# Experts' loops on one core: bounds loaded once, addresses computed early, loop hints, and gate and up as 256 columns with the sum over channels in two banks

## The reference, cut to what matters

```
expert of a token: the best of 4 groups, in it the 2 best of 8 experts   (1024 tokens, 32 experts)
hid = silu(x @ w_gate[e]) * (x @ w_up[e])      # x 1024 channels, hid 512
y   = hid @ w_down[e]                          # 1024 channels
out = sum over a token's two experts of weight * y
```

## Time and profile before

| | |
|---|---|
| median of three runs | 4520.54 us |
| the profiled execution | 4520.74 us, its span 4519.0 us |
| TensorE busy | 3849.0 us, 85% |
| VectorE busy | 1608.9 us, 36% |
| ScalarE busy | 905.4 us, 20% |
| granted TensorE clock, mean | 0.959 |
| DMA, mean over the span | 143 GB/s |
| first to last record of L2387 and L2396, layer 0 | 2471 to 3157 us |
| the same, layer 1 | 3746 to 4434 us |

### The profile page before, as it was taken

One profiled execution on the slowest core, in us unless ns is written; L12 is line 12 of the kernel. 1 busy time (PEld: TensorE's weight loads), 2 busy tenths in 40 slices (PEclk: granted clock), 3 DMA queues, 4 the chain that ended last, 5 costly groups with the idle time before them and its releaser, 6 DMA issues.

```text
span 4519.0 us, 113553 instructions
## 1 busy us (share of the span) xinstructions
PE 3849.0 (85%) x45324; PEld 2478.6 (55%) x45325; DVE 1608.9 (36%) x3673; ACT 905.4 (20%) x2284; POOL 271.6 (6%) x453
## 2 busy tenths in 40 slices
PE   6997888999998899999897777777699987877774
PEld 3564665554445554446644666666444446766664
DVE  2676666223106641524634222222411142222214
ACT  3013444111003321311522111111200021111111
POOL 0000000000000000000001111111100002111111
PEclk9998999999999999999998999999799998999997
DMA  8101223002100001102413778885300225778784
GB/s 318 38 19 57 94 96 120 22 24 68 39 37 1 1 10 47 45 30 94 164 44 139 297 319 326 347 337 217 112 37 37 76 97 234 296 288 364 322 348 141
DMA packets 94346, 644.30 MB, mean 143 GB/s; under 512 B 18640, under 2 KB 41240, under 8 KB 60752
## 3 DMA queue, kind: packets, MB, share of 16 engines
q10 hardware_dynamic: 28896, 386.28, 20.5%
q1 hardware_dynamic: 46928, 194.98, 11.6%
q0 software_dynamic: 18336, 60.44, 4.1%
HBM read 594.70 MB, written 46.92 MB: 142 GB/s over the span
## 4 chain that ended last, share of the span: by engine, by line
PE 48%; issue 5%; DVE 4%; DVEq 2%; DMA 2%; ACT 1%; POOLq 0%; POOL 0%; SPq 0%; ACTq 0%
PE banks L258 22%; PE banks L2387 14%; PE banks L2396 7%; DVEq L2290 1%; DMA arena<-y_tok,arena 1%; PE banks L2382 1%; PE banks L1519 1%; PE banks L2378 1%; DVE arena L2525 1%; DVE arena L1634 1%; PE banks L2118 1%; DVEq L2525 1%; DMA h_tok<-arena 0%; PE banks L467 0%; PE banks L1568 0%
## 5 line engine op out<-in xcount | busy, mean ns | idle before, releaser
L258 PE MATMUL banks<-arena 128*128 128x512 f32 (+2 forms) x4544 | 1749.4, 546 | 38.8 <-ACTq L137 16.9
L258 PEld LDWEIGHTS banks<-arena 128*128 128x128 f32 x4544 | 840.3, 191 | 935.9 <-issue 885.0
L2387 PE MATMUL banks<-arena 128*32 128x128 f32 x20480 | 658.7, 280 | 138.2 <-issue 130.2
L2387 PEld LDWEIGHTS banks<-arena 128*32 128x32 f32 x20480 | 571.9, 112 | 208.4 <-issue 206.7
L2396 PE MATMUL banks<-arena 128*32 128x128 f32 x10240 | 341.7, 290 | 168.6 <-DVE arena L2525 168.3
L2396 PEld LDWEIGHTS banks<-arena 128*32 128x32 f32 x10240 | 301.8, 117 | 207.5 <-issue 206.4
L2490 DVE COPY arena<-banks 128x128 f32 x162 | 47.2, 291 | 491.4 <-PE banks L2382 488.2
L1588 PE MATMUL banks<-arena 128*64 128x128 f32 x1952 | 161.7, 284 | 55.1 <-ACT arena L1601 39.4
L945 DVE SCALAR_TENSOR_TENSOR arena<-arena 128x1024 f32<-128x1024 f32 x240 | 195.9, 878 | 0.2 <-DVEq L137 0.2
L2353 POOL DMA_INDIRECT arena<-h_tok,arena x176 | 171.9, 977 | 142.2 <-POOL arena L2350 136.5
L301 DVE SCALAR_TENSOR_TENSOR arena<-banks,arena 128x512 f32<-128x512 f32 (+1 forms) x72 | 51.9, 721 | 333.2 <-PE banks L258 333.2
(11 more groups left out here) (327 smaller groups left out, 3257.6 us busy)
## 6 DMA issues: line engine op xcount, KB each, us to landing
arena<-in_w_gu ACTq DMA_DIRECT2D x120, 2048.0 KB, 7.4
arena<-in_w_dn ACTq DMA_DIRECT2D x60, 2048.0 KB
arena<-in_w_ada SPq DMA_DIRECT2D x24, 2048.0 KB, 7.3
y_tok<-arena SPq DMA_DIRECT2D x648, 32.0 KB
arena<-in_w_gu SPq DMA_DIRECT2D x8, 2048.0 KB, 9.2
y_tok<-arena POOLq DMA_DIRECT2D x1, 12800.0 KB, 36.0
arena<-in_ab_w_ada SPq DMA_DIRECT2D x6, 2048.0 KB, 9.7
arena<-in_cd_w_ada SPq DMA_DIRECT2D x6, 2048.0 KB, 7.2
```

What stands on the lines that cost most here:

```text
L258: last = pe.matmul(self.bank_of(g, n), lhsT, rhs, start=k == 0, stop=k == KT - 1)
L2387: last = pe.matmul(bank(2 + part)[32 * q:32 * q + 32, 0:128], xbT[:, 128 * j + 32 * q2:128 * j + 32 * q2 + 32], w_gu[slot][part][:, 2 * q2 ...
```

## The change

The weights of gate and up are laid out anew on the host: unit j holds the channels of half j for all columns, 256 columns (128 of gate, 128 of up) for each strip. A matmul streams 256 columns, a block has 32 instead of 64 of them. The sum over the channels ends in two banks: half 0 in bank 2, half 1 in bank 3. ScalarE copies bank 2 to gu_part, VectorE adds bank 3 to it, ScalarE takes SiLU of 128 columns, VectorE multiplies 128 columns. Addition, SiLU and product of block b - 1 now all stand in turn b. In the loops VectorE computes addresses ahead of its waits (snap), and bounds are loaded once and handed on as registers. TensorE's loops have the hint at the back edge. ScalarE issues the gate/up loads when half 1 of the last block is done.

```diff
-        w_gu = [[mem(a + UNIT * h, KT, 4, 128) for h in range(2)] for a in SLOTS]
+        w_gu = [[mem(a + UNIT * j, 16, 256) for j in range(2)] for a in SLOTS]
+        gu_part = mem(HT + 4992, 256)
+        gu_sum = mem(HT + 5248, 256)
...
             def in_turn(self, eng, first, second):
-                first(0, 0)
+                c0, c1 = self.cum(eng, 0), self.cum(eng, 1)
+                first(0, 0, c0, c1)
                 with eng.Fori(0, E // 2 - 2) as p:
-                    first(2 * p + 1, 1, p)
-                    second(2 * p, 0, p)
-                    first(2 * p + 2, 0, p + 1)
-                    second(2 * p + 1, 1, p)
+                    c1, c2 = self.cum(eng, 2 * p + 1), self.cum(eng, 2 * p + 2)
+                    first(2 * p + 1, 1, c1, c2, p)
+                    c0 = self.cum(eng, 2 * p)
+                    second(2 * p, 0, c0, c1, p)
+                    c3 = self.cum(eng, 2 * p + 3)
+                    first(2 * p + 2, 0, c2, c3, p + 1)
+                    second(2 * p + 1, 1, c1, c2, p)
...
+            def trips(self, eng, begin, end):
+                return nc.Fori(begin, end, engines=bass.OrderedEngineSet([eng.engine]), hint_back_edge=True)
...
-            def gu_half(self, pe, slot, part, j):
+            def gu_half(self, pe, slot, j):
                 for q2 in range(4):
                     for q in range(4):
-                        last = pe.matmul(bank(2 + part)[32 * q:32 * q + 32, 0:128],
-                                         xbT[:, 128 * j + 32 * q2:128 * j + 32 * q2 + 32], w_gu[slot][part][:, 2 * q2 + j, q],
-                                         start=j == 0 and q2 == 0, stop=j == 1 and q2 == 3, tile_position=(0, 32 * q),
+                        last = pe.matmul(bank(2 + j)[32 * q:32 * q + 32, 0:256],
+                                         xbT[:, 128 * j + 32 * q2:128 * j + 32 * q2 + 32], w_gu[slot][j][:, 4 * q2 + q],
+                                         start=q2 == 0, stop=q2 == 3, tile_position=(0, 32 * q),
                                          skip_group_check=True)
...
                 def gate_up(i, slot, begin, end, nth=None):          # TensorE
...
+                    with self.trips(pe, begin, end) as b1:
                         pe.wait_ge(self.x0, b1)
-                        pe.wait_ge(self.ma, b1)
-                        self.gu_half(pe, slot, 0, 0)
+                        pe.wait_ge(self.pc, b1)
+                        self.gu_half(pe, slot, 0).then_inc(self.g0, 1)
+                        pe.wait_ge(self.mu, b1)
+                        self.turn_hid(pe)
                         pe.wait_ge(self.x1, b1)
-                        self.gu_half(pe, slot, 0, 1).then_inc(self.ga, 1)
-                        pe.wait_ge(self.mb, b1)
-                        self.turn_hid(pe)
                         pe.wait_ge(self.xr[1], b1)
                         self.turn_x(pe).then_inc(self.xt[1], 1)
-                        self.gu_half(pe, slot, 1, 0).then_inc(self.gb0, 1)
-                        self.gu_half(pe, slot, 1, 1).then_inc(self.gb, 1)
+                        self.gu_half(pe, slot, 1).then_inc(self.g1, 1)
...
             def blocks_act(self, a):
+                def silu(b1):
+                    a.wait_ge(self.ad, b1)
+                    return a.activation(sg, gu_sum[:, 0:128], ACT.Silu).then_inc(self.si, 1)
+
+                def gate_up(i, slot, begin, end, nth=None):
+                    with a.Fori(begin, end) as b1:
+                        silu(b1)
+                        a.wait_ge(self.g0, b1)
+                        a.activation(gu_part, bank(2)[:, 0:256], ACT.Copy).then_inc(self.pc, 1)
+                    a.wait_ge(self.g1, end)
+                    a.sem_inc(passed, 1)
...
             def blocks_dve(self, d):
+                def add(b1):
+                    d.wait_ge(self.g1, b1)
+                    d.wait_ge(self.pc, b1)
+                    d.tensor_tensor(gu_sum, gu_part, bank(3)[:, 0:256], ALU.add).then_inc(self.ad, 1)
+
+                def times(b1):
+                    d.wait_ge(self.si, b1)
+                    d.tensor_tensor(hid, sg, gu_sum[:, 128:256], ALU.mult).then_inc(self.mu, 1)
+
+                def gate_up(i, slot, begin, end, nth=None):
+                    with d.Fori(begin, end) as b1:
+                        add(b1)
+                        self.turned_half(d, 1).then_inc(self.x1, 1)
+                        times(b1)
+                        self.keep_hid(d, b1)
+                        d.wait_ge(self.he, b1)
+                        d.wait_ge(self.xt[1], b1)
+                        self.turned_half(d, 0).then_inc(self.x0, 1)
+                        at = d.snap(((b1 + 1) & (XB - 1)) * 256)
+                        d.wait_ge(self.x_ok[2], b1)
+                        d.tensor_copy(xr, xb[:, bass.ds(at, 256)]).then_inc(self.xr[1], 1)
...
                 def down(i, slot, begin, end, nth=None):             # VectorE
                     with d.Fori(begin, end) as b1:
-                        at = ((b1 + 1) & (HELD - 1)) * 128
+                        at = d.snap(((b1 + 1) & (HELD - 1)) * 128)
                         d.wait_ge(self.dm, b1)
```

More of the change, by code:

```diff
@@ L2407, in blocks_pe @@
                 self.turn_x(pe).then_inc(self.xt[0], 1)
-                def gate_up(i, slot, nth=None):
+                def gate_up(i, slot, begin, end, nth=None):
                     nth = i // 2 if nth is None else nth
-                    begin, end = self.cum(pe, i), self.cum(pe, i + 1)
                     pe.wait_ge(self.wa[slot], 16 * nth + 16)
@@ L2464, in gate_up, with down @@
                             self.load_gu(a, slot, e, part)
-                def down(i, slot, nth=None):
-                    with a.Fori(self.cum(a, i), self.cum(a, i + 1)) as b1:
-                        room = (b1 & (XB - 1)) * 256
+                def down(i, slot, begin, end, nth=None):
+                    with a.Fori(begin, end) as b1:
+                        room = a.snap((b1 & (XB - 1)) * 256)
                         a.wait_ge(self.yf, b1)
@@ L2476, in down @@
                         self.load_dn(a, slot, self.expert(a, i + 2))
-                self.in_turn(a, gate_up, down)
-                down(E - 1, 1)
-                top = self.cum(a, E)
+                begin, top = self.in_turn(a, gate_up, down)
+                a.wait_ge(self.ad, top)
+                a.sem_inc(passed, 1)
+                silu(top)
+                down(E - 1, 1, begin, top)
                 for half in (self.y0, self.y1):
@@ L2488, in keep_hid @@
             def keep_hid(self, d, b1):
+                at = d.snap((b1 & (HELD - 1)) * 128)
                 d.wait_ge(self.ht, b1)
-                d.tensor_copy(held[:, bass.ds((b1 & (HELD - 1)) * 128, 128)], bank(4)[:, 0:P]).then_inc(self.he, 1)
+                d.tensor_copy(held[:, bass.ds(at, 128)], bank(4)[:, 0:P]).then_inc(self.he, 1)
             def blocks_dve(self, d):
                 d.sem_inc(self.yf, 6)
-                d.sem_inc(self.ma, 1)
+                d.sem_inc(self.g1, 1)
                 d.sem_inc(self.dm, 1)
@@ L2509, in gate_up @@
+                def times(b1):
+                    d.wait_ge(self.si, b1)
+                    d.tensor_tensor(hid, sg, gu_sum[:, 128:256], ALU.mult).then_inc(self.mu, 1)
+                def gate_up(i, slot, begin, end, nth=None):
+                    with d.Fori(begin, end) as b1:
+                        add(b1)
+                        self.turned_half(d, 1).then_inc(self.x1, 1)
+                        times(b1)
                         self.keep_hid(d, b1)
-                        d.wait_ge(self.sa, b1)
@@ L2527, in down @@
                         d.tensor_copy(hidS[:, 64:128], held[:, bass.ds(at + 64, 64)]).then_inc(self.h1, 1)
-                self.in_turn(d, gate_up, down)
-                top = self.cum(d, E)
-                d.wait_ge(self.sb, top)
-                d.sem_inc(passed, 1)
-                d.tensor_tensor(hid[:, 64:128], sg[:, 64:128], bank(3)[:, 64:128], ALU.mult).then_inc(self.mb, 1)
+                begin, top = self.in_turn(d, gate_up, down)
+                add(top)
+                times(top)
                 self.keep_hid(d, top)
```

52 lines of the change are left out of this document (16 added, 36 removed).

## The result

The changed kernel takes **4354.97 us** (median of 4 runs, 4341.51 to 4363.8), against 4523.07 for the kernel before: ratio 0.9626, 95% interval 0.9596 to 0.9656. The forecast was 4316, in a range of 4265 to 4400. The profiled execution took 4360.02 us, its span is 4358.2 us.

A forecast was written before the change was run, and what follows sets the result against it. No engine is full; TensorE's 22% idle, at loop changes and a piece after the gather, was the prize. Columns 6, idle piece 45, loop changes 123, addresses 21, clock 20, less loads 10: 205 off 4520.7 gives 4316 us, range 4265 to 4400.

The forecast's parts named there:

- Columns and idle piece: Gate/up turns: 256-column matmuls save 6 us, and the longer queue bridges TensorE's idle piece after the gather, 45 us.
- Changes of loop: Between gate/up and down loops: fewer bound loads and VectorE leaving the gate/up loop earlier save 123 us.
- The late ScalarE: Light gate/up to heavy down: ScalarE issues two weight loads first, returns y late, costing the second down block 0.35 us.
- Early addresses: Down loop: the address of held computed ahead of VectorE's wait removes 0.22 us per further block, 21 us.
- The hint: Jump back of TensorE's loops: named with the early addresses, but given no saving or cost of its own.
- Clock: Phases behind changes of loop: about half the clock dips vanish with the shorter idle, 20 us back.
- Loads: Expert weight loads: pairs with 4 blocks outrun the DMA queues, so 10 us are subtracted from the gain.
- A to E: Five rivals: gather's idle stays; hid late; loads bind; strips not side by side; engines enter the next loop no earlier.
- A: Rival, gate/up turns: the queue does not bridge the idle piece after the gather; 4361 us, chance 0.15.
- E: Rival, loop changes: standalone waits stop engines entering the next loop earlier, only removed work counts; 4415 us, chance 0.07.
- B: Rival, gate/up turns: hid comes late and an engine's chain becomes the bound; 4364 us, chance 0.10.

The follow-up runs named there:

- e4: The changed kernel with bounds loaded as before and without the hint, leaving 256 columns and the new order: 4377.62 us, ratio 0.9678.
- e2: The kernel before, with GpSimd gathering no rows in the second layer after its first eight groups: 4493.01 us, ratio 0.9935.
- e3: The kernel before, with only the bounds loaded once and handed on, 4 loads a pair instead of 8: 4434.3 us, ratio 0.9804.
- e5: The changed kernel without the hint for the jump back, all else the same: 4331.76 us, ratio 0.9576.
- e9: The changed kernel without the hint, GpSimd's gather waiting for the first half of a later gate/up turn: 4337.55 us, ratio 0.959.
- e2b: The changed kernel, with GpSimd gathering no rows in the second layer: 4346.33 us, ratio 0.9611.
- e11: The changed kernel without the hint, ScalarE loading the next expert's index ahead of its wait for the last gate/up matmul: 4281.48 us, ratio 0.9547.
- e6n: The changed kernel without the hint, with VectorE's and ScalarE's down-loop addresses put in registers ahead of the wait: 4327.77 us, ratio 0.9571.
- e1: The kernel before, with only the jump-back hint added to TensorE's two inner loops: 4565.55 us, ratio 1.0095.
- e12: e11 with bounds carried in registers from pair to pair and VectorE's address in a register ahead of the wait: 4251.74 us, ratio 0.948.
- e7: The changed kernel, with the hint, ScalarE's expert weight loads moving half the bytes: 4345.19 us, ratio 0.961.
- e13: e12 with ScalarE's expert weight loads moving half the bytes: 4230.03 us, ratio 0.9354.

## Why the prediction was right, and where its sizes were not

Forecast 205 us off, measured 161 between the profiled executions (4520.7 and 4360.0), 168 between the medians. The stages lost 168; the rest of the program took 7.5 us more. The two large terms and their mechanisms hold, 52 and 119 us measured where 51 and 123 were forecast; the addresses and the clock, 41 us, came to nothing. Of the 44 us missing the addresses are 21, the clock 22.5, the changes 4 and the rest of the program 7.5; against them stand 10 forecast for the loads, whose waits lie inside the changes, and 1 of the columns.

- **Columns and idle piece, 51 us: right.** Turns of 4.07 (4.05 forecast); without phases at the lower clock the gate/up sums fall by 52. e4 shows that the hint has no part in it, e2 that the gather was the cause. That a longer queue bridges the stall fits after and e4, but was not tested by itself.
- **Changes of loop, 123 us: 133.5 measured, 119 like for like.** Idle and tail together: 0.80, 1.36 and 0.20 where I had 0.9, 1.4 and 0.65, and 2.39 where I had 2.28. But my 0.65 held 0.35 for the late ScalarE, which the trace has in the down phases (next point). The part title was misleading: of the gain the bounds are one half (e3, 71 us), the new order of VectorE's work the other (e4, 72 us), and the hint takes 12 back (e5).
- **The late ScalarE: right place, too small.** I had 0.35 at the second down block. It costs 0.53 in a phase of four blocks (8.75, 8.22 before), covered in part by the gather's piece: the wait has ScalarE's load of the next expert's number in it, which I had left out of that sum. Down phases without clock losses grew by 14.5 us in sum instead of shrinking by 21. e9, e2b and e11 settle this.
- **Early addresses, 21 us: failed.** "The address of held is computed ahead of the wait" is not what the kernel does. The chain has the three instructions behind the wait as before; naming a value early emits nothing. e6n shows that moving them removes the bubble, and that then ScalarE is next, so alone it is worth 4 us, not clear of nothing, where I had 21.
- **The hint, nothing: failed.** It stands in every turn and hides there, as forecast. What the forecast left out is the entry to a loop, where nothing hides it: 0.1 us at each of 60 entries to a gate/up loop. All changes together are 12 us longer with it in the kernel after, and with the clock it costs 23 us there (e5) and 43 in the kernel before (e1).
- **Clock, 20 us back: failed.** The phases lose as much to it as before (71.5 and 74.1 us over the shortest phase of the same length; ScalarE's waits are in it too). The heavy gate/up, behind the one change of loop that the edit leaves at 2.1, is where it still falls: 21 of the 62 gate/up phases begin at the lower clock in after (their first 32 records take over 2.2 us from first to last start, 1.7 elsewhere), 13 without the hint (e5), 12 before. In e12, where that change is 1.44, only 7 do: the first of either layer and five behind changes of 4.3 to 7.8.
- **Loads, 10 us: no more than that.** e7 is 10 us faster, but is not clear of noise.

Rivals: A to E did not occur as a whole. E is true for the addresses only. The range's upper end is said to be A and B together; those make 4409, not 4400, which changes nothing here.

**The version to build.** e12 answers to four of these: no hint, ScalarE's index ahead of its wait, VectorE's address in a register ahead of its wait, bounds carried from pair to pair.

## What to carry to other kernels

When a gap between two loops closes, look at every engine that does something at that boundary, also those that issue loads for later: their work was free only as long as the gap lasted. Idle charged to one cause may cover another; a run that removes the first and leaves the time as it is tells it. Where the kernel before has another time than usual, compare phases in the traces before ratios: a stall may be missing there. And read in the instruction stream whether an early address or a hint is there at all, and what it is, before pricing it.

## What was not expected of the hardware

- TensorE starts no products for about 0.5 us while GpSimd sets off a gather: the piece ends 1.27 to 1.35 us after the DMA_INDIRECT begins, and is gone without it (e2). It isn't always there: it is absent from the heavy down phases of e11 and e12 and present in those of e13, with the gather, and in e12 ScalarE's weight issues too, at the same place. What else it needs is open.
- A hint for the jump back costs about 0.1 us at each entry to a loop whose start waits for TensorE's sequencer, and nothing inside the loop; with it the granted clock of a stretch was 0.95 in place of 0.98 (e1).
- A load of one bound into a register costs its engine 0.5 to 0.7 us, all told (e3); ScalarE's load of an expert's number, 0.28 and what follows it, was half a microsecond of the wait in each heavy down phase (e11).
